# Two-block transformer kernel: both delta-rule chains of the mixer in the same beats, and the gated unit's first channel between the two sixes of query, key and value slabs

## The chip, the cores and the metric

One core of a Trainium2 chip runs the whole program. The metric is the device time of one execution in microseconds (us), the median over runs. The engines are named as the profile names them: PE (TensorE, matrix products), PEld (its weight loads), DVE (VectorE), ACT (ScalarE), POOL (GpSimd) and SP (SyncE, which issues the DMAs).

## The reference, cut to what matters

Input x is 512 tokens of 1024 features, float32. Two blocks follow one another. The first is a hybrid mixer, a cross attention to 256 memory tokens and a gated feed-forward net with a short convolution; the second is a retention layer and a stick-breaking attention layer. The change is in the mixer of the first block only:

```python
z = h @ w_in                                    # qkv (1536), gate, a/b logits, cfm_in (1024)
qkv = silu(causal_dwconv(qkv, gdn_conv_w))      # 4 taps, 12 tiles of 128 features
q, k = l2norm(q), l2norm(k)                     # 4 heads of 128
g = -exp(a_log) * softplus(a_logit + dt_bias); beta = sigmoid(b_logit)
o = gated_delta_rule_chunked(q, k, v, g, beta)  # chunks of 64 tokens:
#   L = strict(beta k k^T * decay); solve (I + L) [u | w] = [beta v | beta k exp(g)]
#   for each of 8 chunks: v_new = u - w S;  o = q exp(g) S + (q k^T * decay) v_new
#                         S = S exp(g_last) + (k exp(g_last - g))^T v_new
o = rmsnorm(o, gdn_norm_g) * silu(gate)
c = causal_dwconv(glu(cfm_in), cfm_dw_w) + cfm_dw_b     # 31 taps, 4 channels of 128 features
c = silu(layernorm(c))
y = concat([o, c]) @ w_out
```

## The kernel before, in words

**Products.** Activations lie with features on partitions and the 512 tokens along the free axis. Every float32 weight slab (128 x 1024, 512 KB) is brought in by SP through three `raw` buffers, rounded to a high part by ACT (`sh`, line 1307) and split into a low part by DVE (`sl`, line 2052), in four slots each. A product of a slab is then three passes (lines 502 to 504) over eight feature tiles, 24 matmuls of 512 columns. The helper `slab` does one slab, `tokens` does four slabs with tokens as the stationary side; small float32 products go through `one` (line 507).

**Order of the work.** It is written out by hand, once for each engine, in `tensor_program`, `scalar_program`, `vector_program` and `pool_program`. An order list (`weight_order`) fixes which slab comes when: slabs 0 to 5 are query, key and value of heads 0 and 1, slabs 6 to 9 the gated unit's channels 0 and 1 (two slabs each), slabs 10 to 15 query, key and value of heads 2 and 3, slabs 16 to 19 the gated unit's channels 2 and 3, slabs 20 to 31 the eight memory-key and four gate slabs in the order of `KEYS_GATES`, slabs 32 to 39 the memory values, slabs 40 to 47 the output projection of the mixer.

**Beats and lanes.** Work other than slabs is written as Python generators that are put into lanes (`bg`, `fg`, `side`; `gp` and `tp` for the 31-tap convolution). At each beat every lane runs its first generator on to the next `yield`. When a generator ends, the next one in its lane starts within the same tick. On PE a slab has three beats (after 9, 18 and 24 of its 24 matmuls), a memory-key slab one, a group of `tokens` two (for two token tiles). Each of the other engines has its own beats written at matching places; the engines meet through semaphores alone, each engine running its own list strictly in order.

**The chains.** `chain(p)` does the delta rule of heads 2p and 2p+1; it takes 37 ticks on PE: k k^T (tick 2), the transposes of v (5 and 6), q k^T and the start of the inverse (7), five doubling levels of two ticks each (8 to 17: 16 products of 64x64 in the first, 32 in the second), keys, u and w (18 to 20), then for each of 8 chunks a tick with w S (`ws`) and one with k^T v_new and the output (`kv`, `o`) (21 to 36), and the transposes back (37, line 820). Chain 0 starts before slab 6 in lane `bg`, chain 1 after slab 14 in lane `fg`. The state `SS` is one tile for both; POOL zeroes it again for chain 1 (line 3063). Each chain has two PSUM banks of its own, `KBANK = ((4, 5), (2, 3))`; the recurrence uses banks 6 and 7 in turn for `ws` and `o`, and one of the chain's own for `kv`. ACT copies each chunk's output out of PSUM (`tok`, line 1458).

**The 31-tap convolution.** Channels 0 and 2 are done by ACT (products, line 1503) and POOL (sums, line 3071). Channels 1 and 3 are done by DVE (lines 2257 and 2262), one tap at each beat of DVE in lane `tp`, two at each beat from the memory keys on, 31 taps each; taps(1) is added behind glu(1), taps(3) behind glu(3). `cfm_norm` is the layer norm behind it. Before the second beat group of the memory values has its split, `tp` is drained.

**The heads' norm.** `gdn_out(p)` has on ACT the squares of the output (first tick, line 1582) and the logarithm and exponential (fourth tick, lines 1590 and 1594); it has five yields there. On DVE it has the sum of squares (second tick, line 2376) and the scaling (sixth tick, line 2381), and six yields. On PE it has a product with ones for each head (third tick), and three yields. gdn_out(0) is added to lane `side` at item 10 of `KEYS_GATES`, gdn_out(1) to lane `fg` after item 11, before the memory values.

Of the kernel before, what the change touches and what calls it, by code (L numbers as in the profile page):

```python
# [9 lines left out]
ALU = mybir.AluOpType  # L10
# [5 lines left out]
EPS = 1e-6  # L16
# [150 lines left out]
def program(nc, A, out):  # L167
    root = ExitStack()
    with root:
# [42 lines left out]
        with ExitStack() as ph:  # L212
# [14 lines left out]
            SS = alloc(ph, "ss", [128, 2, 128])  # L227
# [189 lines left out]
        def tap_sum(c, q):  # L417

            return ACC[:, c, :] if q == 30 else PS[TAP_BANKS[0] if c == 1 and q < TAP_HOP else TAP_BANKS[1]][:]
# [36 lines left out]
        GLB = ((1, 2), (0, 1), (0, 1), (0, 1))  # L456
# [31 lines left out]
        def tensor_program(e):  # L488
# [127 lines left out]
            for _ in range(8):  # L616
                one(PS[7][:, 0:256], SS[:, 0, :], SS[:].rearrange("p a b -> p (a b)"), True, True)

# [67 lines left out]
            def chain(p):  # L686
# [103 lines left out]
                for n in range(8):  # L790
                    tb, par = n // 2, n % 2
                    R, RO = RR[par], RR[1 - par]
                    b = bank(6 + par)
                    pe.wait_ge(*gac[(p, "wq", par)])
                    pe.wait_ge(*(gdv[(p, "s", n - 1)] if n else ggp[(p, "s0")]))
                    for h in range(2):
                        g = (h * 8 + n) * 128
                        t = one(b[:, h * 128:h * 128 + 128], W2[:, g:g + 128], SS[:, h, :], h == 0, False)
# [24 lines left out]
                rel[6], rel[7] = [(gac, (p, "ot", 0))], [(gac, (p, "ot", 1))]  # L823

            def mem():
                b = bank(3)
# [6 lines left out]
                rel[3] = [(ms, "mem")]  # L833
# [3 lines left out]
                one(bank(3)[:, 0:256], ONE[:], DG[:, 0:256], True, True).then_inc(*rw("mem"))  # L837
                rel[3] = [(rb, "mem")]
# [9 lines left out]
            bg.add(chain(0))  # L848

# [18 lines left out]
            rel[TAP_BANKS[1]] = [(tpd, (3, 30))]  # L868
# [37 lines left out]
            fg.drain()  # L906
            fg.add(gdn_out(1))
# [2413 lines left out]
```

## Time and profile before

| | |
|---|---|
| median of 3 runs | 1692.43 us (1691.57 to 1696.03) |
| time of the profiled execution | 1691.26 us |
| its span, first to last instruction | 1689.5 us |
| PE busy | 1673.6 us (99%) in 9421 matmuls |
| PE weight loads | 1404.4 us (83%) |
| DVE busy | 1047.3 us (62%) |
| ACT busy | 739.1 us (44%) |
| POOL busy | 187.3 us (11%) |
| mean granted clock of PE | 0.999 of full speed |

The span is that of the one profiled execution; its own time is 1.8 us more. Busy times of PE are modelled: matmuls overlap in the pipeline, so the distance between the starts of two matmuls says more than their lengths. A line x16 or x32 can hold two records for each small float32 product. The number in brackets at a line's end is the idle time before it and what ended it.

### The profile page before, as it was taken

How to read it: one execution, taken by the hardware profiler on the slowest of the kernel's cores; microseconds unless marked ns; L12 is line 12 of the kernel's file. 1: busy time of each engine (PE TensorE's matmuls, PEld its weight loads, DVE VectorE, ACT ScalarE, POOL GpSimd, SP SyncE). 2: the span in 40 equal slices, each digit the busy share in tenths (PEclk: the TensorE clock that was granted, in tenths of full speed). 3: DMA queues.
4: the chain of work that ended last, by engine and by line, in shares of the span. 5: the costliest groups of instructions: out<-in, count | busy, mean ns of one | idle time of the engine just before them, and what ended most of it. 6: DMA issues, size and time to landing. Idle time of an engine off the chain costs nothing.

```text
span 1689.5 us, 23254 instructions
## 1 busy us (share of the span) xinstructions
PE 1673.6 (99%) x9421; PEld 1404.4 (83%) x9421; DVE 1047.3 (62%) x1565; ACT 739.1 (44%) x1137; POOL 187.3 (11%) x163
## 2 busy tenths in 40 slices
PE   9999999999999999999999999999999999999998
PEld 7787887987898888888888888888898888888887
DVE  7889787474389449549675642655574545454445
ACT  6654467653553323213543323323364645253463
POOL 0455461200200000000100000000100000000001
PEclk9999999999999999999999999999999999999999
DMA  6111134421223223322322313313222222222221
GB/s 216 62 43 63 51 101 135 137 78 50 75 67 121 100 75 113 101 86 100 119 88 80 96 56 106 100 57 112 69 72 76 75 76 87 75 87 76 85 77 50
DMA packets 45576, 147.67 MB, mean 87 GB/s; under 512 B 5024, under 2 KB 8992, under 8 KB 45472
## 3 DMA queue, kind: packets, MB, share of 16 engines
q1 hardware_dynamic: 45472, 146.21, 26.5%
q8 instruction: 75, 1.23, 0.3%
q14 instruction: 29, 0.24, 0.0%
HBM read 144.09 MB, written 2.10 MB: 87 GB/s over the span
## 4 chain that ended last, share of the span: by engine, by line
PE 88%; DVE 8%; ACT 2%; issue 1%; DMA 0%; POOL 0%; SPq 0%; DVEq 0%; ACTq 0%
PE ps L502 22%; PE ps L504 22%; PE ps L503 22%; PE ps L507 21%; DVE sl L2052 1%; DVE ps L2112 1%; DVE y L2467 1%; DVE xl L2484 1%; DVE h L2477 0%; PE ps L1128 0%; ACT sh L1307 0%; DVE ps L2262 0%; DVE ps L2106 0%; DVE pad L2104 0%; DMA raw<-in_wqkv 0%
## 5 line engine op out<-in xcount | busy, mean ns | idle before, releaser
L1307 ACT ACTIVATE sh<-raw 128x1024 fp32r<-128x1024 f32 x257 | 268.3, 1053 | 373.1 <-PE ps L504 254.4
L2052 DVE TENSOR_TENSOR sl<-raw,sh 128x1024 fp32r<-128x1024 f32 x257 | 321.6, 1258 | 131.5 <-ACT sh L1307 131.4
L502 PE MATMUL ps<-xh,sh 128*128 128x512 f32 (+1 forms) x664 | 263.1, 396 | 0.0
L504 PE MATMUL ps<-xl,sh 128*128 128x512 f32 (+1 forms) x664 | 254.0, 382 | 0.0
L503 PE MATMUL ps<-xh,sl 128*128 128x512 f32 (+1 forms) x664 | 253.7, 382 | 0.0
L502 PE MATMUL ps<-sh,xh 128*128 128x512 f32 x384 | 151.8, 395 | 0.0
L503 PE MATMUL ps<-sh,xl 128*128 128x512 f32 x384 | 149.6, 390 | 0.0
L504 PE MATMUL ps<-sl,xh 128*128 128x512 f32 x384 | 149.6, 390 | 0.0
L502 PEld LDWEIGHTS ps<-xh,sh 128*128 128x128 f32 x664 | 124.9, 188 | 26.2 <-issue 2.4
L504 PEld LDWEIGHTS ps<-xl,sh 128*128 128x128 f32 x664 | 124.8, 188 | 24.9
L503 PEld LDWEIGHTS ps<-xh,sl 128*128 128x128 f32 x664 | 125.0, 188 | 22.7 <-issue 0.7
L3002 POOL TENSOR_TENSOR dg<-dg,sq 128x512 f32<-128x512 f32 (+1 forms) x27 | 30.1, 1116 | 828.4 <-ACT sq L1313 827.2
L502 PE MATMUL ps<-x2hu,sh 128*128 128x256 f32 (+1 forms) x346 | 118.4, 342 | 0.0
L504 PE MATMUL ps<-x2lu,sh 128*128 128x256 f32 (+1 forms) x346 | 115.8, 335 | 0.0
L503 PE MATMUL ps<-x2hu,sl 128*128 128x256 f32 (+1 forms) x346 | 115.1, 333 | 0.0
L502 PE MATMUL ps<-x2hd,sh 128*128 128x512 f32 (+1 forms) x300 | 103.7, 346 | 0.1
L504 PE MATMUL ps<-x2ld,sh 128*128 128x512 f32 (+1 forms) x300 | 102.4, 341 | 0.0
L503 PE MATMUL ps<-x2hd,sl 128*128 128x512 f32 (+1 forms) x300 | 102.1, 340 | 0.0
L3071 POOL TENSOR_TENSOR acc<-acc,ca 128x512 f32<-128x512 f32 x60 | 86.0, 1433 | 68.9 <-ACT ca L1503 64.5
L504 PEld LDWEIGHTS ps<-sl,xh 128*128 128x128 f32 x384 | 72.1, 188 | 15.6
L502 PEld LDWEIGHTS ps<-sh,xh 128*128 128x128 f32 x384 | 72.1, 188 | 15.2 <-issue 0.5
L503 PEld LDWEIGHTS ps<-sh,xl 128*128 128x128 f32 x384 | 72.1, 188 | 15.2 <-issue 0.5
(429 smaller groups left out, 3317.5 us busy)
## 6 DMA issues: line engine op xcount, KB each, us to landing
raw<-in_wup SPq DMA_DIRECT2D x44, 512.0 KB, 3.5
raw<-in_wdn SPq DMA_DIRECT2D x24, 512.0 KB, 3.5
raw<-in_rqk SPq DMA_DIRECT2D x16, 512.0 KB, 3.9
raw<-in_rv SPq DMA_DIRECT2D x16, 512.0 KB, 3.4
raw<-in_rg SPq DMA_DIRECT2D x16, 512.0 KB, 4.4
raw<-in_rout SPq DMA_DIRECT2D x16, 512.0 KB, 3.5
raw<-in_sv SPq DMA_DIRECT2D x16, 512.0 KB, 3.4
raw<-in_sg SPq DMA_DIRECT2D x16, 512.0 KB, 3.5
```

The lines of the kernel that those rows point to most:

```text
L502: e.matmul(dst, wh, ah, start=start, stop=False, skip_group_check=True)
L503: e.matmul(dst, wl, ah, start=False, stop=False, skip_group_check=True)
L504: return e.matmul(dst, wh, al, start=False, stop=stop, skip_group_check=True)
L507: return e.matmul(dst, a, b, start=start, stop=stop, skip_group_check=True)
L1307: e.activation(SH[j % NSPL][:], RAW[j % NRAW][:], ACT.Copy).then_inc(*hi(j))
L2052: e.tensor_tensor(SL[j % NSPL][:], RAW[j % NRAW][:], SH[j % NSPL][:].bitcast(F32), ALU.subtract).then_inc(*lo(j))
L2112: e.scalar_tensor_tensor(C[:], PAD[:, 1 + q:1 + q + T], prm("gconv", tile * 4 + q), C[:], ALU.mult, ALU.add).then_inc(*cv((n, "t", q) if q ...
L2467: e.scalar_tensor_tensor(Y[:, k, c], Y[:, k, c], prm(gpost[0], gpost[1] + k), PS[0][:, 0:256] if b == 5 and hf else YR[:, c], ALU.mult, AL ...
L2484: e.scalar_tensor_tensor(lo_[:, k, c], H[:, k, c], prm(g[0], g[1] + k), hi_[:, k, c].bitcast(F32), ALU.mult, ALU.subtract).then_inc(*s2((k ...
L3002: e.tensor_tensor(SA[:, c], SA[:, c], SQ[(k - 1) % 2][:] if k < 4 else half(SQ, k % 4), ALU.add).then_inc(*sa(("y", b, k)))
L3071: e.tensor_tensor(ACC[:, c, :], ACC[:, c, :], gpb[("tmp", c, q)], ALU.add).then_inc(*tpp((c, q)))
```

## The change

Both chains are added to their lanes at the same place, after slab 12 (`JOIN = 10`, the slab of the conv tile n = 10). The gated unit's channel 0 keeps slabs 6 and 7; channel 1 moves behind the second six, which move two slabs forward (slabs 8 to 13; glu(1) has 14 and 15). Each chain has a state of its own, zeroed at the start. `ws` and `o` use the chain's own second bank for every chunk in place of banks 6 and 7 in turn. The DVE taps have one bank, 7, and no change of bank. The memory's sums move from bank 3 to 6. The chains are drained, and both gdn_out are put into lane `side`, at item 9 of `KEYS_GATES` (`HEADS_OUT = 9`). Nothing is computed otherwise than before.

```diff
 weight_order:
-        for c in (2 * p, 2 * p + 1):
+        for c in ((0,), (1, 2, 3))[p]:
             o += [("wcfm", 4 + c), ("wcfm", c)]
...
-            SS = alloc(ph, "ss", [128, 2, 128])
+            SSP = [alloc(ph, f"ss{i}", [128, 2, 128]) for i in range(2)]
...
-        ONB = ((4, 3), (6, 7))
-        TAP_BANKS, TAP_HOP = (2, 5), 12
-        CVB = (0, 1, 2, 3, 5, 0, 0, 1, 0, 1, 0, 1)
+        ONB = ((4, 5), (2, 3))
+        TAP_BANK, JOIN, HEADS_OUT = 7, 10, 9
+        CVB = (0, 1, 2, 3, 5, 0, 1, 0, 1, 0, 1, 0)
-        GLB = ((1, 2), (0, 1), (0, 1), (0, 1))
+        GLB = ((1, 0),) * 4
 PE, chain(p):
-                    b = bank(6 + par)
+                    b = bank(B_)
...
-                    rel[6 + par] = [(gac, (p, "tok", n))]
+                    rel[B_] = [(gac, (p, "tok", n))]
                     yield
                 for h in range(2):
-                    b = bank(6 + h)
+                    b = bank(KBANK[p][h])
 PE, main order:
-            bg.add(chain(0))
             glu(0, 6)
             side.add(mem())
-            glu(1, 8)
-            rel[TAP_BANKS[0]] = [(tpd, (1, TAP_HOP))]
             for n in range(6, 12):
-                slab(4 + n, X, "x", beats=3, at_bank=[n % 2])
-                rel[n % 2] = [(cva, conv_tile(n))]
-                if n == 10:
+                slab(n + 2, X, "x", beats=3, at_bank=[CVB[n]])
+                rel[CVB[n]] = [(cva, conv_tile(n))]
+                if n == JOIN:
+                    bg.add(chain(0))
                     fg.add(chain(1))
+            glu(1, 14)
             glu(2, 16)
             glu(3, 18)
...
-            bg.drain()
             side.drain()
             for i, (kind, n) in enumerate(KEYS_GATES):
-                if i == 10:
+                if i == HEADS_OUT:
+                    bg.drain()
+                    fg.drain()
                     side.add(gdn_out(0))
+                    side.add(gdn_out(1))
...
-            fg.drain()
-            fg.add(gdn_out(1))
             bg.add(cfm_norm())
 ACT and DVE: the same moves of chain, glu(1), gdn_out and drains
 DVE, taps(c):
+                        ve.wait_ge(*dca[("ea", 1, 1)])
...
-                        if c == 1 and q == TAP_HOP:
-                            ve.wait_ge(*gac[(0, "w", 1)])
 POOL:
-            e.memset(SS[:], 0.0).then_inc(*ggp((0, "s0")))
+            e.memset(SSP[0][:], 0.0).then_inc(*ggp((0, "s0")))
+            e.memset(SSP[1][:], 0.0).then_inc(*ggp((1, "s0")))
...
-                if p:
-                    po.wait_ge(*gdv[(0, "s", 6)])
-                    po.wait_ge(*gmm[(0, "o", 7)])
-                    e.memset(SS[:], 0.0).then_inc(*ggp((1, "s0")))
```

## Rows read from the trace of the kernel before

**Rows 1.** The page, part 1: busy time, share of the span and instructions of each engine.

```profile
PE 1673.6 (99%) x9421; PEld 1404.4 (83%) x9421; DVE 1047.3 (62%) x1565; ACT 739.1 (44%) x1137; POOL 187.3 (11%) x163
```

**Rows 2.** Waits of PE: who waited for whom; us in total, times, longest.

```profile
PE ps L706 <- DVE u_xq L2167: 1.3, 1, 1.3
PE ps L507 <- DVE km L2179: 1.1, 1, 1.1
...
PE ps L820 <- ACT qk L1458: 0.9, 2, 0.6
```

**Rows 3.** PE timeline: a stretch of slabs alone; start, length, engine, line, operation, tiles.

```profile
41.09 0.39 PE L502 MATMUL ps<-xh,sh 128*128 128x512 f32 x1
...
44.27 0.39 PE L504 MATMUL ps<-xl,sh 128*128 128x512 f32 x1
```

**Rows 4.** PE timeline: chain 0's doubling levels between pieces of slabs.

```profile
79.96 1.15 PE L507 MATMUL ps<-u_xq,u_x 64*64 64x64 f32 x32
...
83.30 1.15 PE L507 MATMUL ps<-km,u_xq 64*64 64x64 f32 x32
84.29 1.10 PE L507 MATMUL ps<-u_xq,km 64*64 64x64 f32 x32
...
86.91 1.15 PE L507 MATMUL ps<-u_xq,u_x 64*64 64x64 f32 x32
```

**Rows 5.** PE timeline: chain 0's recurrence alone, then sharing a beat with chain 1.

```profile
120.33 0.61 PE L507 MATMUL ps<-ss,u_xq 128*128 128x128 f32 x4
...
122.96 0.71 PE L507 MATMUL ps<-qk,u_x 64*128 64x128 f32 x4
...
126.38 0.60 PE L507 MATMUL ps<-ss,u_xq 128*128 128x128 f32 x4
...
152.50 0.71 PE L507 MATMUL ps<-qk,u_x 64*128 64x128 f32 x4
...
153.71 0.66 PE L706 MATMUL ps<-idn,u_rq 128*128 128x128 f32 x4
```

**Rows 6.** DVE timeline: the first operations of two successive convolution tiles.

```profile
24.37 0.69 DVE L2104 TENSOR_TENSOR pad<-ps,rb 128x512 f32<-128x512 f32 x1 [1.56 <-ACT rb L1387]
...
29.27 0.68 DVE L2104 TENSOR_TENSOR pad<-ps,rb 128x512 f32<-128x512 f32 x1
```

**Rows 7.** POOL timeline: one of the chain's masks.

```profile
65.09 1.30 POOL L3045 TENSOR_TENSOR u_l<-u_a,ch 128x512 f32<-128x512 f32 x1
```

**Rows 8.** ACT timeline: one copy of a chunk's output.

```profile
240.05 0.38 ACT L1458 ACTIVATE qk<-ps 64x256 f32<-64x256 f32 x1 [1.04 <-PE ps L507]
```

**Rows 9.** DVE timeline: two taps, and the operations around the start of the memory values.

```profile
242.42 1.53 DVE L2262 SCALAR_TENSOR_TENSOR ps<-cp,prm,ps 128x512 f32<-128x512 f32 x2
...
263.95 0.42 DVE L2408 TENSOR_TENSOR km<-ps,cm 128x256 f32<-128x256 f32 x1
264.30 1.21 DVE L2052 TENSOR_TENSOR sl<-raw,sh 128x1024 fp32r<-128x1024 f32 x1
267.61 1.30 DVE L2376 TENSOR_TENSOR sq<-sq,q 128x512 f32<-128x512 f32 x2 [2.09 <-ACT sq L1582]
268.82 0.74 DVE L2381 SCALAR_TENSOR_TENSOR qk<-qk,prm,dg 128x512 f32<-128x512 f32 x1
...
271.28 0.68 DVE L2389 TENSOR_TENSOR gt<-qk,gt 128x512 f32<-128x512 f32 x1
```

**Rows 10.** Windows at the end: us, PE, PEld, DVE, ACT, POOL busy, PEclk, DMA share, GB/s.

```profile
1685.50:1686.00 0.50, 0.05 (x1) 0.00 (x0) 0.50 (x3) 0.38 (x1) 0.00 (x0) 1.00 1.03 342
...
1687.00:1689.47 2.47, 0.00 (x0) 0.00 (x0) 0.00 (x0) 0.00 (x0) 0.00 (x0) 0.50 0.63 211
```

**Rows 11.** PE timeline: the eight float32 products (256 columns) at the start, two later.

```profile
1.10 5.25 PE L507 MATMUL ps<-ss 128*128 128x256 f32 x16 [1.10 <-POOL ss L3017]
...
326.25 0.59 PE L507 MATMUL ps<-dg,one 128*128 128x256 f32 x2
326.68 0.59 PE L507 MATMUL ps<-sq,one 128*128 128x256 f32 x2
```

More of the change, by code:

```diff
@@ L417, in tap_sum @@
         def tap_sum(c, q):
-            return ACC[:, c, :] if q == 30 else PS[TAP_BANKS[0] if c == 1 and q < TAP_HOP else TAP_BANKS[1]][:]
+            return ACC[:, c, :] if q == 30 else PS[TAP_BANK][:]
         RS = (DG[:], PAD[:, 0:T])
@@ L616, in tensor_program @@
             for _ in range(8):
-                one(PS[7][:, 0:256], SS[:, 0, :], SS[:].rearrange("p a b -> p (a b)"), True, True)
+                one(PS[7][:, 0:256], SSP[0][:, 0, :], SSP[0][:].rearrange("p a b -> p (a b)"), True, True)
             for i, k in FIRST:
@@ L797, in chain @@
                         g = (h * 8 + n) * 128
-                        t = one(b[:, h * 128:h * 128 + 128], W2[:, g:g + 128], SS[:, h, :], h == 0, False)
+                        t = one(b[:, h * 128:h * 128 + 128], W2[:, g:g + 128], SSP[p][:, h, :], h == 0, False)
                     t.then_inc(*gmm((p, "ws", n)))
@@ L822, in chain @@
                 yield
-                rel[6], rel[7] = [(gac, (p, "ot", 0))], [(gac, (p, "ot", 1))]
+                rel[A_], rel[B_] = [(gac, (p, "ot", 0))], [(gac, (p, "ot", 1))]
             def mem():
-                b = bank(3)
+                b = bank(6)
                 for _ in range(9):
@@ L836, in mem @@
                 pe.wait_ge(*dg["mem"])
-                one(bank(3)[:, 0:256], ONE[:], DG[:, 0:256], True, True).then_inc(*rw("mem"))
-                rel[3] = [(rb, "mem")]
+                one(bank(6)[:, 0:256], ONE[:], DG[:, 0:256], True, True).then_inc(*rw("mem"))
+                rel[6] = [(rb, "mem")]
                 yield
@@ L1523, in scalar_program @@
             ahead(10)
-            bg.add(chain(0))
+            conv_act(4)
+            beat(3)
+            conv_act(5)
             def glu(c, j):
-                if c == 0:
-                    conv_act(4)
-                beat(2 if c == 2 else 3)
+                beat(2 if c < 2 else 3)
                 ahead(j + 5)
-                if c == 0:
-                    conv_act(5)
                 ac.wait_ge(*glv[(c, "sg")])
@@ L1541, in scalar_program @@
             side.add(mem())
-            glu(1, 8)
             for n in range(6, 12):
                 beat(2 if n > 6 else 3)
-                ahead(9 + n)
-                if n == 10:
+                ahead(n + 7)
+                if n == JOIN:
+                    bg.add(chain(0))
                     fg.add(chain(1))
@@ L1549, in scalar_program @@
                 conv_act(n)
+            glu(1, 14)
             glu(2, 16)
@@ L1608, in mem_v @@
                                  ACT.Copy, scale=LNC[:, 2 + tb:3 + tb]).then_inc(*vma((cg, tb)))
-            bg.drain()
             side.drain()
             for i, (kind, n) in enumerate(KEYS_GATES):
-                if i == 10:
+                if i == HEADS_OUT:
+                    bg.drain()
+                    fg.drain()
                     side.add(gdn_out(0))
+                    side.add(gdn_out(1))
                 if kind == "mk":
@@ L2236, in mem @@
                 ve.wait_ge(*cs["m"])
-                e.tensor_scalar(LNC[:, 0:2], PS[3][:, 0:2], 1.0 / 1024, EPS, ALU.mult, ALU.add).then_inc(*ms("mem"))
+                e.tensor_scalar(LNC[:, 0:2], PS[6][:, 0:2], 1.0 / 1024, EPS, ALU.mult, ALU.add).then_inc(*ms("mem"))
                 yield
@@ L2301, in glu @@
             def glu(c, j):
-                beat(3 if c % 2 else 2)
+                beat(2 if c < 2 else 3)
                 ve.wait_ge(*used[j])
@@ L2324, in vector_program @@
             side.add(mem())
-            glu(1, 8)
             for n in range(6, 12):
                 beat(2 if n > 6 else 3)
-                if n == 10:
+                if n == JOIN:
+                    bg.add(chain(0))
                     fg.add(chain(1))
-                conv(n, 4 + n, n % 2, beat)
-                low(8 + n)
+                conv(n, n + 2, CVB[n], beat)
+                low(n + 6)
+            glu(1, 14)
             glu(2, 16)
@@ L2395, in head_lo @@
                     *x2l(("2mix", k)))
-            bg.drain()
             side.drain()
             for i, (kind, n) in enumerate(KEYS_GATES):
-                if i == 10:
+                if i == HEADS_OUT:
+                    bg.drain()
+                    fg.drain()
                     side.add(gdn_out(0))
+                    side.add(gdn_out(1))
                 if kind == "mk":
@@ L3088, in pool_program @@
             beat(3)
-            bg.add(chain(0))
-            for c in range(2):
+            for c in range(4):
+                if c == 1:
+                    for n in range(6, 12):
+                        beat(3)
+                        if n == JOIN:
+                            bg.add(chain(0))
+                            fg.add(chain(1))
                 beat(6)
@@ L3095, in pool_program @@
                     gp.add(taps(c))
-            for n in range(6, 12):
-                beat(3)
-                if n == 10:
-                    fg.add(chain(1))
-            for c in (2, 3):
-                beat(6)
-                if c in ON_GP:
-                    gp.add(taps(c))
-            bg.drain()
             side.drain()
```

21 lines of the change are left out of this document (9 added, 12 removed).

## The prediction

> **What bounds the kernel now.** I read the page first: PE is busy for 99% of the span [rows 1], so a time can only come from PE's own work growing or shrinking, or from holes. The view of waits, taken for PE alone, shows how small the holes are: the longest is 1.3 us, where the chain's second transposes wait for DVE; then 1.1 us for the start of the inverse, and 0.9 us at the transposes back [rows 2]. Then I read PE's timeline through the mixer, for the distances between starts. In a slab alone 14 steps take 44.27 - 41.09 = 3.18 us [rows 3], 0.227 us for each 512-column matmul; nine between two beats take 2.04. Whatever a beat takes beyond that is what its chain work costs, the change from one kind of product to the other included.
>
> **Part 1: sharing beats saves changes.** A first half of a level costs 83.30 - 79.96 - 2.04 = 1.30 us. A second half has 6 matmuls behind it (1.36): 86.91 - 83.30 - 1.36 = 2.25 [rows 4]. Within that beat the second set of 16 products starts 0.99 us after the first, so a set costs 0.99 when it follows another and the rest, 0.27 to 0.31, is entering and leaving float32. With both chains in a beat that rest is paid once: 10 level beats by 0.29 = 2.9 us. In the recurrence `ws` costs 122.96 - 120.33 - 2.04 = 0.59, `kv` and `o` together 126.38 - 122.96 - 2.04 = 1.38; where chain 1's transposes follow `kv` and `o` in the same beat, they start after 153.71 - 152.50 = 1.21 [rows 5]. So 8 beats by 0.17 = 1.4. For `ws` no such pair is used here; it lies between nothing and 0.17, nearer nothing, since two wide float32 products fill most of the 0.59: 8 by 0.05 = 0.4. The other eight beats (k k^T, two of transposes, q k^T, keys, u, w, back) lie between 0.1 and 0.3: 8 by 0.17 = 1.4. Together 6.1. But seven beats are shared already, chain 0's last and chain 1's first; by the same prices they now save 7 by 0.2 = 1.4. And three pieces of side work (decay rows, a memory sum) ride in chain 0's beats now and stand alone after: 3 by 0.2 = 0.6. **Saved: 6.1 - 1.4 - 0.6 = 4.1 us**, bounds 2.5 and 6.
>
> **Part 2: slabs ahead of the chains.** Slabs 8 to 13 come one behind another and alternate between banks 0 and 1, so slab n+2 waits for the convolution of slab n. DVE takes 29.27 - 24.37 = 4.90 us for a convolution and a split [rows 6], PE 24 by 0.227 = 5.45 for a slab. The eight memory splits (a quarter of a slab's split each, under 0.5 us) come in the first three of these slabs and take the margin away: three slabs by 4.9 + 1.3 against 5.45 is 2.3 us behind, of which DVE's head start of under two us is taken off. **0.5 us lost**, bounds 0 and 1.5. The DMAs keep order and number; only four slabs change places with six others, and the issue on SP hangs on the splits as before. Losing POOL's second zeroing and its two waits costs nothing: it is done at the start, ahead of the first product.
>
> **Part 3: the chains' start, twice in the same beats.** The two waits of 1.3 and 1.1 us [rows 2] come from DVE and POOL working through norms, masks and scaling between ticks 2 and 7. Now both chains ask for that at once. POOL's masks double (a mask is 1.30 [rows 7]), DVE's chain work (seven operations on a 512-column tile at 0.68 [rows 9] and some small ones, about 5.5 us) becomes 11, beside one convolution and two splits, 4.9 + 1.2 [rows 6]. PE has, from k k^T to the inverse, five pieces of slab (about 10.2) and 4 to 5 us of chain work. There are no taps on DVE at that time, since taps(1) starts behind glu(1); that is the cover. I get PE to the second transposes 1.9 us early and to chain 1's inverse 0.7 early. 2.6 us lost against 2.4 for chain 0 and about 0.8 for chain 1 now: **0.6 us won**, bounds 2 won and 3 lost.
>
> **Part 4: one bank for `ws` and `o`.** Before, `ws` of a chunk needed the copy of two chunks ago, now that of the last. The copy takes 0.38 [rows 8] and there is a piece of slab of 2.04 us, or a memory-key slab, between `o` and the next `ws`. ACT reaches the copy in time except where a Silu of a gate tile stands ahead of it, which waits for DVE, which has six taps to do: I take **0.7 us lost** in all, bounds 0 and 14 waits by 0.5, 7.
>
> **Part 5: the end of the chains.** Both have done 36 ticks by item 9 and the last one is drained without a slab over it; ACT copies chain 0's output between chain 0's transposes back and chain 1's. About 1.5 us, where now two waits at the transposes, 0.9 together [rows 2], and one of 0.5 before them stand. Nothing, within 1.
>
> **Part 6: gdn_out(0) and gdn_out(1) in one lane.** This is the dear one. In one lane the second starts when the first has ended, and the first is three yields long on PE and six on DVE. Count ticks from item 9: items 9, 10, 11 have 1, 3, 1, so the memory values start with tick 6. PE's product for gdn_out(1) is in tick 3 + 3 = 6, after the first six matmuls of slab 32. DVE's sum of squares, which it needs, is in tick 6 + 2 = 8, in the second group. PE stands in order and waits. Behind the end of slab 31 DVE still has: the evacuation of item 11, 0.42; a split, 1.2; gdn_out(0)'s scaling, 2 by 0.7; four taps (channel 3's are not through: 12 + 16 + 24 = 52 of 62 taps fit before), 2 by 1.45; a split, 1.2; head_out(0), 0.6; the first sum, 0.65 [rows 9]. That is 8.4 us. PE has six matmuls to do in that time, 1.36. **7.0 us lost**, bounds 6.5 (DVE quite up to date when slab 31 ends) and 8.5 (it is over a us late). Before, both generators started at the same beat on every engine, and no wait is seen there. Nothing gives it back later: the ten taps moved to this place (7.3 us of DVE) are then hidden under the wait, and without the wait they would not be free either.
>
> **Part 7: the clock.** PE's last product ends at 1685.55, and from 1687.0 on the granted clock is 0.50, half of 2.4 GHz [rows 10]; so a hole of 7 us should see it fall. What it costs to come back: the eight first products take 5.25 us, and two such products later start 326.68 - 326.25 = 0.43 apart, 3.4 for eight [rows 11]. **1.8 us lost**; bounds 0 (it does not fall) and 2.6 (all 5.25 at half speed). The Trainium skill says the same from the other side: "TensorE: Matmul & The Clock Gate", under "Why this matters for your kernels", warns against idle gaps between bursts of matmuls since the clock then drops. By that rule the sum stands; if it did not hold for this hole the sum would be 1.8 less.
>
> **The sum.** -4.1 + 0.5 - 0.6 + 0.7 + 0 + 7.0 + 1.8 = +5.3 us. Against the profiled execution's own 1691.26 that is 1696.6; that execution lies 1.2 under the median of 1692.43, so I forecast 1692.4 + 5.3 = **1697.7 us**, 0.31% slower. A measurement of this kernel can tell about 0.3%, 5.1 us, from no change; my sum stands just on that line.
>
> **Rivals.** (a) *The clock holds* through the hole: +3.5, 1695.9, within 0.3%. Against it stands the fall 1.45 us after the last product [rows 10]. (b) *No hole:* DVE reaches tick 8 in time, or the two lanes' counts meet by something that I misread; then parts 6 and 7 go and the result ends on the other side, -3.5, 1688.9. It decides at the third group of six matmuls in slab 32: if PE passes it without a wait, this is the case. For it speaks only that waits now are small everywhere. If the sharing saved its upper bound too, it would be -5.4, 1687.0. (c) *Waits all through the shared beats:* each `ws` waits for a copy just asked for, each `kv` for DVE, which has up to two taps and both chains to serve in a beat of a memory-key slab (about 4.2 us of work for 4.2 to 5.6 of PE). 14 bank turns by 0.5 less the 0.7 counted: +11.6, 1704. Against it: ACT waits 1.04 us for PE just before such a copy [rows 8], so it is not behind there. The Trainium skill would point here: "Trainium Kernel Development and Optimization", "Best Practices", reads regular bubbles as a sign that PSUM buffers ran out, and this change halves them for `ws`. No bubble is seen with two banks, so the trace cannot decide it.
>
> **Chances.** The forecast's mechanism with the clock falling 0.50, of it 0.32 above 5.1 and 0.18 below; (a) 0.14, all within; (b) 0.20, of it 0.11 beyond 5.1 with savings at their bound and 0.09 within; (c) 0.16, all slower. So slower 0.48, within 0.3% 0.41, faster 0.11. The range goes from 1688.5 (no hole, savings as taken) to 1703 (the forecast and half of (c)); beyond it lie the better half of (b) and the worse half of (c).
>
> **What would show it.** In the changed trace: x32 groups of both chains 0.99 apart in the same beat; PE's view of waits led by one of about 7 us, the product with ones (line 507, `sq`, `one`) waiting for DVE line 2376's tile, just after the start of the memory values; the granted clock below 1 in the window behind it; PE reaching slab 32 some 3 to 4 us earlier than now if parts 1 to 5 are right. I am wrong in part 6 if that wait is under 3 us, in part 1 if the start of slab 32 has not moved forward, in part 4 if waits on line 1458 add up to more than 2 us.

## The result, and the profile after

The changed kernel takes **1728.74 us** (median of 4 runs, 1727.64 to 1732.31) against 1693.32 (1691.57 to 1696.03) of the kernel before on the same chip: ratio 1.0216, 95% interval 1.0205 to 1.0228. It is 2.2% slower, 35 us, where 5 us were forecast. The direction was right, the size was not, and the time lies far outside the range.

The page of the changed kernel, its span, part 1 and two rows of part 2; it answers to [rows 1].

```profile
span 1727.6 us, 23250 instructions
PE 1683.4 (97%) x9421; PEld 1415.1 (82%) x9421; DVE 1055.1 (61%) x1565; ACT 745.7 (43%) x1142; POOL 183.3 (11%) x163
PE   9889997999999999999999999999999999999998
PEclk9999898999999999999999999999999999999999
```

The profiled span grew by 1727.6 - 1689.5 = 38.1 us. PE has the same 9421 products but is busy 9.8 us longer, and idle 28.3 us longer. Everything happens in slices 2 to 8, the mixer; two digits of the clock's row are 8 there, and no slice of the kernel before shows less than 9. So two things have to be found: idle time and a slower clock.

The view of waits for PE alone; us in total, times, longest. It answers to [rows 2].

```profile
PE ps L507 <- DVE sq L2371: 9.1, 1, 9.1
PE ps L502 <- ACT u_xq L1395: 5.0, 1, 5.0
PE ps L706 <- DVE u_xq L2164: 4.3, 1, 4.3
PE ps L820 <- ACT qk L1456: 3.3, 2, 2.2
PE ps L507 <- DVE sl L2049: 2.7, 5, 1.0
PE ps L502 <- DVE cp L2312: 2.6, 1, 2.6
PE ps L502 <- ACT qk L1395: 2.1, 1, 2.1
PE ps L507 <- DVE dg L2054: 1.5, 1, 1.5
PE ps L507 <- DVE sq L2356: 1.5, 1, 1.5
...
PE ps L507 <- DVE u_t L2176: 1.0, 1, 1.0
PE ps L507 <- POOL msum L3073: 1.0, 1, 1.0
```

The first row is the hole that was predicted at gdn_out(1), 9.1 us instead of 7.0. The second (slab 7 waits for the Silu of convolution 5), the sixth (slab 20 waits for DVE's work on slab 19, channel 3 of the gated unit) and the seventh (a slab waits for a convolution's Silu) are turns of a PSUM bank in the slabs; of these the prediction has only the last one's kind, at 0.5 us. The third is the chains' start, the fourth their end.

The granted clock is best read in windows laid on the stretches where it is at 0.50, here with one of 1.00 ahead of the third (columns: window, length, PE, PEld, DVE, ACT, POOL busy, PEclk, DMA share, GB/s).

```profile
61.90:65.30 3.40, 3.40 (x8) 2.72 (x9) 0.00 (x0) 2.80 (x3) 0.00 (x0) 0.51 0.32 130
120.20:126.80 6.60, 5.65 (x17) 4.41 (x17) 5.92 (x8) 2.95 (x3) 6.31 (x5) 0.50 0.26 79
191.00:195.00 4.00, 4.00 (x40) 3.56 (x39) 0.41 (x1) 1.04 (x2) 1.26 (x1) 1.00 0.36 126
195.40:205.40 10.00, 9.76 (x43) 8.76 (x42) 0.55 (x2) 6.83 (x12) 1.82 (x2) 0.50 0.00 1
209.00:212.00 3.00, 3.00 (x16) 3.00 (x15) 0.00 (x0) 0.00 (x0) 0.94 (x1) 0.50 0.59 180
273.60:276.80 3.20, 3.03 (x14) 3.04 (x15) 1.21 (x2) 1.80 (x6) 0.00 (x0) 0.50 0.54 169
300.30:304.20 3.90, 3.89 (x5) 1.83 (x6) 3.76 (x6) 0.00 (x0) 0.00 (x0) 0.50 0.32 122
```

The clock falls to 1.2 GHz, half of 2.4, six times. PE works in these windows for 3.4 + 5.7 + 9.8 + 3.0 + 3.0 + 3.9 = 28.8 us; at half speed about half of that, **14.4 us**, is lost. Now the balance closes: 28.3 us of idle time and 14.4 of clock make 42.7, and the span grew by 38.1, so the sharing of beats saved about **4.6 us**.

Five of the falls stand at a wait. The third does not. PE's timeline there (start, length, engine, line, operation, tiles) shows `w` of chain 0 and, right behind it, `w` of chain 1:

```profile
191.88 3.06 PE L507 MATMUL ps<-km,u_xq 64*128 64x64 f32 x29
...
195.05 5.55 PE L507 MATMUL ps<-u_t,u_rq 64*128 64x64 f32 x29
```

29 products of the same shape took 3.06 us and then 5.55, with PE never idle.

**Where the sharing did save.** PE's timeline in a level of both chains, which answers to [rows 4]:

```profile
134.59 1.15 PE L507 MATMUL ps<-u_xq,u_x 64*64 64x64 f32 x32
135.57 1.10 PE L507 MATMUL ps<-u_rq,u_r 64*64 64x64 f32 x32
...
138.19 1.15 PE L507 MATMUL ps<-km,u_xq 64*64 64x64 f32 x32
139.17 1.10 PE L507 MATMUL ps<-u_xq,km 64*64 64x64 f32 x32
140.10 1.10 PE L507 MATMUL ps<-u_t,u_rq 64*64 64x64 f32 x32
```

Two sets start 0.98 and 0.93 apart. The pair of first halves costs 138.19 - 134.59 less six wide products (1.36) = 2.24, where twice 1.30 was paid.

### The profile page after: what moved, and what is told of

Its sections match the earlier page's. It is cut to its first block, busy times and chain, and to the rows that moved or that the text cites. A ratio compares the mean times of both kernels' runs of the same rounds, so it can differ in the third digit from the quotient of the medians.

```text
span 1727.6 us, 23250 instructions
## 1 busy us (share of the span) xinstructions
PE 1683.4 (97%) x9421; PEld 1415.1 (82%) x9421; DVE 1055.1 (61%) x1565; ACT 745.7 (43%) x1142; POOL 183.3 (11%) x163
## 4 chain that ended last, share of the span: by engine, by line
PE 84%; DVE 9%; ACT 3%; issue 2%; DMA 0%; SPq 0%; POOL 0%; DVEq 0%; ACTq 0%; POOLq 0%
PE ps L502 21%; PE ps L504 21%; PE ps L503 21%; PE ps L507 20%; DVE sl L2049 2%; DVE ps L2109 1%; DVE y L2462 1%; DVE ps L2258 1%; DVE xl L2479 1%; ACT sh L1305 1%; DVE h L2472 0%; PE ps L1126 0%; DMA acc<-in_xT 0%; DVE ps L2103 0%; DVE u_xq L2085 0%
## 5 line engine op out<-in xcount | busy, mean ns | idle before, releaser
L504 PEld LDWEIGHTS ps<-sl,xh 128*128 128x128 f32 x384 | 72.1, 188 | 15.7
```

The source lines that it names most:

```text
L504: return e.matmul(dst, wh, al, start=False, stop=stop, skip_group_check=True)
```

## The experiments

PE's idle time at each place and the clock give the candidates; each of these kernels takes one away. The first five are each one edit of the changed kernel.

**1. gdn_out(1) in its old lane.** The same edit on PE, ACT and DVE:

```diff
                     side.add(gdn_out(0))
-                    side.add(gdn_out(1))
...
                 rel[i % 2] = [(kmv if kind == "mk" else gtv, n)]
+            fg.add(gdn_out(1))
             bg.add(cfm_norm())
```

> The changed kernel, with gdn_out(1) put back into lane fg behind item 11 on PE, ACT and DVE, so that its ticks are counted alike again. In the changed kernel PE waited 9.1 us for it and the clock was at half for 10.2 us from that wait on. My theory: the wait was the lanes' miscount and nothing else, so the time falls by 9.1 for the wait and 1 to 2 for the clock, to about 1718. Rival: DVE is late there anyhow, with ten taps moved in, and the wait comes back under the names of splits and sums; then it falls by 2 to 4 only, to about 1725.

Measured: 1727.91 us (1723.51 to 1728.49), ratio to the kernel before 1.0204 (1.0189 to 1.022). By the ratios that is 0.12%, 2 us, and the intervals overlap: removing the largest hole is worth next to nothing. The waits of PE from the memory values to the output projection in this kernel:

```profile
PE ps L507 <- DVE u_l L2342: 4.8, 1, 4.8
PE ps L507 <- DVE sq L2371: 1.6, 1, 1.6
PE ps L502 <- DVE km L2404: 1.2, 1, 1.2
```

The hole is gone and 7.6 us stand elsewhere: DVE is behind, and PE now meets that at the channel sums (line 2342). So the lane's count decided where PE stopped, not how long. What makes DVE late there is a separate question; run 8 is about it.

**2. Slab 7 in bank 2, as before.**

```diff
-        GLB = ((1, 0),) * 4
+        GLB = ((1, 2),) + ((1, 0),) * 3
```

> The changed kernel, with the second slab of the gated unit's channel 0 in bank 2 as before, in place of bank 0. Theory: its wait of 5.0 us for ACT's Silu of convolution 5 goes, and with it the fall of the clock for 3.4 us behind it (1.7 us of work), so 6 to 7 us less, about 1722. Rival: the stretch of slabs 8 to 13 is bound by DVE and the wait only moves to their banks; then at most 2 us less, about 1727.

Measured: 1727.10 (1724.52 to 1727.74), 1.0202 (1.0187 to 1.0218). The 5.0 us wait is gone and the chains start 4.8 us earlier (k k^T at 102.06 instead of 106.86), but in the profiled run the clock stays at half for 17 us around `w` instead of 10, and about half of the gain is lost there.

**3. The memory's split and sums behind slab 13.** `side.add(mem())` goes from ahead of convolution 6 to behind convolution 11 on all four engines.

```diff
             glu(0, 6)
-            side.add(mem())
             for n in range(6, 12):
...
+            side.add(mem())
             glu(1, 14)
```

> The changed kernel, with the memory's norm started behind slab 13 and not before slab 8, on all engines. Theory: between slabs 8 and 13 DVE is full with convolutions and splits, and the memory's work makes PE wait 1.0 + 1.5 us by itself and 2.1 us at a bank; these go, but part of it comes back at the start of the chains, where DVE is behind already: 2 to 4 us less, about 1726. Rival: it comes back whole, 1729 or more, since the chains' start waits for DVE and POOL more than slabs 8 to 13 do.

Measured: 1726.69 (1726.05 to 1729.06), 1.0205 (1.019 to 1.0221). The chains start 6.3 us earlier (100.59): the 2.1, 1.5 and 1.0 us waits in slabs 8 to 13 are gone, and PE's own memory products have moved behind slab 13 as well. About half of it comes back: the second transposes wait 5.3 us instead of 4.3, the start of the inverse 1.5 instead of 1.0, and the memory's diagonal costs 1.4 at its new place.

**4. Both lanes drained in turns** instead of chain 0 and then chain 1.

```diff
-                    bg.drain()
-                    fg.drain()
+                    while bg.todo or fg.todo:
+                        bg.tick()
+                        fg.tick()
```

> The changed kernel, with the two chains drained by turns (one tick each) in place of one after the other, on PE, ACT and DVE. Theory: chain 1's last copy no longer stands behind chain 0's transposes on ACT, so that of the 3.3 us of waits at the transposes back about 1.5 go: 1727. Rival: the waits are ACT's two splits and taps ahead of the copies and stay; 1729, no change.

Measured: 1727.78 (1726.74 to 1728.32), 1.0208 (1.0191 to 1.0225). Of the two waits at the transposes back (2.2 and 1.1) the second is gone. It is 1 us, less than the runs can tell.

**5. Chain 1 one beat behind chain 0**, on every engine, by a generator that yields once first.

```diff
-                    fg.add(chain(1))
+                    fg.add(later(chain(1), 1))
```

> The changed kernel, with chain 1 one beat behind chain 0 on every engine (one empty tick ahead of it). Every beat still holds work of both. Theory A: the clock falls at 195 us since the two w products of 64 by 64 and 128 columns follow one another for 8.6 us without a slab between them; with a piece of slab between them it does not fall there, about 4 us less, and the wait of 4.3 us at the second transposes gets smaller by 1 to 2; one more tick is drained without cover, 1 us more. Together 1723. Theory B: the clock there answers to the sum of chain work over the whole stretch; no gain from it, 1728 to 1730.

Measured: 1725.81 (1723.89 to 1727.02), 1.0204 (1.0186 to 1.0221). Over the beats of `w` the window's clock is 1.00:

```profile
190.00:210.00 20.00, 20.00 (x168) 17.81 (x167) 9.86 (x18) 11.12 (x20) 7.01 (x5) 1.00 0.09 28
```

The recurrence starts 6.4 us earlier (196.90 against 203.25; part of that only because w(1) now comes after it), and the wait at the second transposes is 3.4 instead of 4.3. But by the ratios the total moves 0.12%, 2 us; the balances behind run 13 show what was lost against it.

**6 and 7. Edits 1 to 4 together, and these with the stagger.**

> The changed kernel with the first four edits together (heads' lane, bank 2, memory behind slab 13, drains by turns). If the four losses are separate they add: 10.5 + 6.5 + 3 + 1.5 = 21.5 less, 1707. If DVE bounds the whole mixer, so that a wait taken away in one place returns in the next, it stays above 1713.

> The same with chain 1 one beat behind chain 0 besides. Theory A of that edit: 4 to 5 us under the run without it, about 1702. Theory B: the same as without it, within 2 us.

Measured: 1714.86 (1711.81 to 1715.17), 1.0132 (1.0117 to 1.0147), and 1712.95 (1711.41 to 1714.16), 1.0125 (1.011 to 1.014). By the ratios the four edits alone are worth 0.12, 0.14, 0.11 and 0.08%, none of them clear of the noise; together they are worth 0.84%, more than their sum of 0.45%. The surplus is not in the waits. In the profiled executions PE is idle 3.9, 5.0, 2.6 and 0.0 us less in runs 1 to 4, 11.5 in all, and 12.7 less in run 6. It is in the clock: the time lost at half clock is 2.2 and 2.7 us more in runs 1 and 2, 1.3 and 2.4 less in runs 3 and 4, and 5.1 less in run 6. Why the clock falls less often once all four waits are gone, no run shows. In run 6 the 4.8 us at the channel sums are still there.

**8. The lane of run 1, and the 62 taps through before the memory values**, by two DVE taps in a beat of channels 2 and 3:

```diff
             def glu(c, j):
-                beat(2 if c < 2 else 3)
+                taps_ = 2 if c > 1 else 1
+                beat(2 if c < 2 else 3, taps_)
...
-                beat(3)
+                beat(3, taps_)
```

> The change, with gdn_out(1) back behind the last gate in the other lane, and with two taps in a beat of VectorE's in the glu of channels 2 and 3, so that the 62 taps are through before the memory values. With the lane alone (the earlier run) the hole of 9.1 us went and 4.8 + 1.6 + 1.2 us of other waits came, and the stretch from the memory tokens to the output projection still took 36.2 us where the kernel before took 25.4. Theory: the ten taps pushed into this stretch are what is left, so with them gone the waits there fall under 2 us, the stretch takes 25 to 29 us and the time is 1716 to 1720 us. Rival: the taps were free there, or cost as much in the glu beats; then the stretch or what is before it keeps the time and the whole is within 2 us of 1727.9.

Measured: 1718.72 (1717.05 to 1720.71), 1.016 (1.0146 to 1.0174). Here the theory held in the time and in the stretch. The stretch of the memory values, in windows of the kernel before, of the changed one and of this one:

```profile
266.00:292.00 26.00, 26.00 (x110) 20.14 (x109) 22.98 (x31) 18.90 (x31) 0.00 (x0) 1.00 0.45 139
```

```profile
289.00:328.00 39.00, 28.39 (x110) 20.73 (x109) 34.37 (x46) 22.80 (x30) 0.13 (x1) 0.87 0.31 99
```

```profile
290.00:316.00 26.00, 25.87 (x106) 19.62 (x107) 24.75 (x33) 22.48 (x30) 0.00 (x0) 1.00 0.47 156
```

The number behind PEld's is DVE's. Before it had 23.0 us of work under 26.0 of PE. The changed kernel puts 12 taps (9.05 us) on top, so DVE needs 34.4, and PE takes 39. Run 1 still has the 12 taps there, 33.8 us of DVE and 36 of PE. With the taps gone as well DVE has 24.8, and the stretch fits into 26 again (315.70 - 289.91 = 25.8 from the first product of the memory values to the first of the output projection; 25.4 before, 38.5 changed). The taps found room in the beats of channels 2 and 3 at little cost: the memory values start at 289.91 instead of 289.57, though the wait at slab 20 is 3.4 us instead of 2.6. Over all the kernels of this study the same stretch takes 38.1 to 38.5 us with the 12 taps and both gdn_out in one lane, 35.4 to 36.3 with the taps and the old lane, and 25.7 to 25.8 with the old lane and no taps. A kernel without the taps but with both gdn_out in one lane was not measured.

**9. All tables of banks as before.**

```diff
-        CVB = (0, 1, 2, 3, 5, 0, 1, 0, 1, 0, 1, 0)
+        CVB = (0, 1, 2, 3, 5, 0, 0, 1, 0, 1, 0, 1)
...
-        GLB = ((1, 0),) * 4
+        GLB = ((1, 2), (0, 1), (0, 1), (0, 1))
```

> The change with the kernel before's tables of banks (slab 7 in bank 2; channels 1 to 3 of the gated unit in banks 0 and 1 in that order, convolutions 6 to 11 in 0, 0, 1, 0, 1, 0 turned to 0, 1, 0, 1 behind slab 8). Theory: the waits of 5.0 us (slab 7 for the Silu of convolution 5) and of 2.6 us (bank 0 asked for by two slabs in a row) go, and with them a fall of the clock or two: 1719 to 1723 us. Rival: the slabs behind wait as much longer for VectorE, which is late there anyway, and the time is within 2 us of 1727.1, the time with slab 7's bank alone.

Measured: 1722.29 (1720.4 to 1723.7), 1.018 (1.0166 to 1.0194). Both waits, 5.0 and 2.6, are gone. The second is the same mistake in another place: with (1, 0) channel 3 leaves slab 19 in bank 0, and slab 20, the first of the memory keys, takes bank 0 too, so its first product waits for DVE to have done with slab 19 (line 2312). The order (0, 1) puts slab 19 in bank 1. By the ratios the time is 0.22%, 3.7 us, under run 2's, of which 2.6 are the wait; for the rest there is the clock, which in this run's profile is at half for 10 us around `w` and not for 17.

**10 and 11. All repairs, and with the stagger.** Edits 1, 3, 4, 8 and 9 together.

> All repairs that leave both chains in the same beats: the banks of before, the memory sums behind slab 13, the drain of both lanes in turns, gdn_out(1) in the other lane, and the 62 taps through before the memory values. Theory (each cost is its own): 1714.9 of the earlier sum of repairs, less 8 to 10 for the taps, less 2 to 4 for the second bank wait: 1701 to 1705 us, still above the kernel before, since both chains' start (4 to 5 us of waits) and the clock's fall in w (10 us at half) stay. Rival: what is repaired comes out as waits elsewhere, since VectorE is what is late: 1709 or more.

> The same as the run before, with chain 1 one beat behind chain 0, so that w of both chains no longer stands back to back. Theory: no clock at half in the w beats, 3 to 5 us less there, 2 us lost again by a longer tail of the chains: 1699 to 1703 us. If it comes out under 1692 the sharing of beats would pay once its side effects are repaired; I do not expect it. Rival: the stagger only moves the waits (the earlier pair differed by 1.9 us): within 1 us of the run before.

Measured: 1701.67 (1700.11 to 1702.65), 1.0058 (1.0044 to 1.0072), and 1703.57 (1702.76 to 1705.24), 1.0073 (1.006 to 1.0085). So of the change's 2.16% the edits around the shared beats take back 1.58%, 27 us, and 0.58%, 10 us, stay. PE's waits in run 10:

```profile
PE ps L706 <- DVE u_xq L2166: 5.3, 1, 5.3
...
PE ps L820 <- ACT qk L1457: 2.2, 1, 2.2
PE ps L507 <- DVE u_t L2178: 1.5, 1, 1.5
PE ps L507 <- DVE dg L2056: 1.4, 1, 1.4
```

The chains' start (5.3 + 1.5, against 1.3 + 1.1 in [rows 2]) and their end are left, and the clock in `w`:

```profile
186.80:196.80 10.00, 10.00 (x48) 9.30 (x47) 0.30 (x1) 6.20 (x11) 1.27 (x1) 0.50 0.00 1
```

The last two kernels are edits of run 10's.

**12. w(1) alone one beat later**, on the base of run 10: chain 1 yields once more between `u` and `w` on PE, ACT and DVE.

```diff
                 yield
+                if p:
+                    yield
                 for par in range(2):
                     b = bank(KBANK[p][par])
```

> The sum of repairs (1701.7 us) with chain 1 one beat behind from its w on, and level with chain 0 before that. Theory: the clock falls in the w beats because both chains' u and w products stand close together; with w(1) one beat later the granted clock stays whole there (10.2 us at half in the sum of repairs), which is 4 to 5 us of PE's time, less about 0.5 to 1 us since ws(0) of chain 1, its transposes back and one ws/o pair no longer share: 1697 to 1699 us. Rival: the fall comes from what is done before, or from the total of such work; then it comes as well, or 10 us later, and the time is 1701 to 1703.

Measured: 1702.3 (1700.03 to 1705.28), 1.0061 (1.0048 to 1.0074): no change. The windows show the clock whole over u, w(0) and what follows, and then one shorter fall behind w(1), again with PE never idle:

```profile
183.30:192.30 9.00, 8.90 (x75) 8.07 (x74) 4.88 (x8) 3.73 (x7) 2.53 (x2) 1.00 0.16 56
192.40:195.80 3.40, 3.40 (x18) 3.40 (x18) 1.16 (x2) 3.32 (x6) 0.51 (x1) 0.54 0.33 96
```

So the long fall comes with the two `w` close together: 10.0 us at half became 3.4, some 3.3 us of PE's time. It was mostly spent again: from w(0) to the first transposes back only 1.0 us is gained (74.5 for 75.5), so 2.3 went into chain 1's recurrence no longer pairing with chain 0's, kind by kind; and the tail from there to the memory values takes 1.1 more (16.9 for 15.8). The theory was right on the cause and wrong on the time.

**13. Both chains one slab later**, on the base of run 10, so that convolution 11 is out of their way:

```diff
-        TAP_BANK, JOIN, HEADS_OUT = 7, 10, 9
+        TAP_BANK, JOIN, HEADS_OUT = 7, 11, 10
```

> The sum of repairs (1701.7 us) with both chains' start one slab later, with the first slab of channel 1, so that convolution 11 and its split are ahead of them and only the gated unit's work stands beside them. The items before the drain are ten instead of nine. Theory: of the 5.3 us wait at the second transposes about half is convolution 11 and the split (5.3 to 2.5), the waits of 1.5 and 1.4 behind it stay: 3 us less, against 1 to 2 us for two more ticks drained with little over them: 1700 to 1702. Rival one, the start is bound by both chains' own small operations beside GpSimd: the wait stays above 4 us and the time is 1703 or more. Rival two, the slabs ahead catch up nothing: same wait, later.

Measured: 1704.84 (1701.62 to 1706.55), 1.0072 (1.0059 to 1.0086). The wait is 4.2 instead of 5.3, the one of 2.2 at the transposes back goes, and two new ones of 2.1 and 2.3 come. The time is what the first rival expected. DVE's timeline ahead of the transposes:

```profile
105.44 1.25 DVE L2154 TENSOR_TENSOR smp<-smp 128x8 f32<-128x8 f32 x1
106.62 0.15 DVE L2155 TENSOR_TENSOR smp<-smp 128x8 f32<-128x8 f32 x1
...
107.44 1.22 DVE L2161 TENSOR_TENSOR smp<-smp,smv 128x8 f32<-128x8 f32 x1
...
108.66 1.01 DVE L2155 TENSOR_TENSOR smp<-smp 128x8 f32<-128x8 f32 x1
...
109.90 1.12 DVE L2161 TENSOR_TENSOR smp<-smp,smv 128x8 f32<-128x8 f32 x1
```

These are eight operations on eight columns, 5.5 us from the first to the end of the last, four of them over 1 us and three 0.15 to 0.17 (the eighth 0.59). The two chains' scaling of norms is stretched here too. The run does not isolate it: convolution 11 is out of the way, but the memory's splits, which start at the same slab, now stand beside it (three before the first transposed tile, 0.87 for two and 1.33 for one). And run 13's idle time is 0.6 us under run 10's; what makes it slower in the profile is the clock.

**The balance of every kernel.** Idle time is what PE is idle more than in the kernel before; clock is half of PE's work in windows laid over each whole fall (for the changed kernel 14.9, where the narrower windows above gave 14.4); what these two exceed the growth of the span by is saved. All in us, from the profiled executions.

| kernel | span | idle time | clock | saved |
|---|---|---|---|---|
| changed | +38.1 | 28.3 | 14.9 | 5.1 |
| runs 1, 2, 3, 4 | +37.2, 36.0, 34.7, 36.6 | 24.5, 23.4, 25.8, 28.4 | 17.1, 17.6, 13.6, 12.5 | 4.4, 5.1, 4.8, 4.3 |
| runs 6, 8, 9, 10 | +20.5, 25.7, 31.8, 10.8 | 15.7, 16.6, 20.8, 7.5 | 9.8, 13.8, 16.3, 8.8 | 5.1, 4.7, 5.3, 5.5 |
| run 13 | +13.1 | 6.9 | 13.0 | 6.8 |
| runs 5, 7, 11 (stagger) | +32.5, 21.0, 12.2 | 24.4, 14.6, 7.1 | 9.3, 9.0, 6.2 | 1.1, 2.6, 1.2 |
| run 12 (w(1) later) | +10.5 | 8.1 | 5.2 | 2.8 |

The last column is a remainder, but a steady one: 4.3 to 5.5 us in nine of the ten kernels whose chains go level, 1.1 to 2.8 where chain 1 is a beat behind, all along or from `w` on. So the stagger gives back clock (2.6 us from run 10 to run 11) and loses most of what sharing beats had saved (4.3 us).

No kernel of this study is faster than the kernel before.

## Why the prediction was wrong

**Part 1 (sharing saves 4.1 us, bounds 2.5 to 6) was right.** The price of [rows 4] carries over, 2.24 for a pair of first halves, and the balance of the span gives 4.6 us. By the prediction's own sign it would be wrong: the start of slab 32 has not moved forward, it comes at 289.57 us instead of 266.00. But that sign holds the costs of parts 2 to 5 and of the clock too, and these are what moved it; the sign was badly chosen. In run 10 the same balance gives the same: idle time grew by 7.3 us over the kernel before, PE did about 17 us of work at half clock (3.4 at 56.8, 3.4 behind the transposes, 10 in `w`), 8.4 lost, and the span is 10.7 longer, so 5.0 saved.

**Part 2 (slabs ahead, 0.5 us) is the step that failed first.** It counted only DVE and named slabs 8 to 13. That slab n+2 waits for the convolution of slab n was right, but the part never looked at who frees slab 7's bank. With (1, 0) slab 7 takes bank 0 from slab 5, whose reader is ACT's Silu of convolution 5, and that stands behind decay's exponentials and a table load. ACT's timeline of the changed kernel:

```profile
59.30 0.63 ACT L1419 ACTIVATE u_a<-u_a 128x512 f32<-128x512 f32 x1
59.95 1.28 ACT L1395 ACT_TABLE_LOAD   x1
61.24 0.60 ACT L1395 ACTIVATE u_xq<-ps 128x512 f32<-128x512 f32 x1
```

PE starts slab 7 at 61.89 after 4.97 us. The diff's line on GLB has no term in the prediction; it was one of its own, 5.0 us at slab 7 and 2.6 at slabs 19 and 20, and the clock behind each. In slabs 8 to 13 the estimate of the memory's splits ("under 0.5 us" each) was low. DVE's timeline there:

```profile
73.55 1.22 DVE L2229 SCALAR_TENSOR_TENSOR x2lu<-gt,prm,x2hu 128x256 fp32r<-128x256 f32 x1 [0.83 <-ACT x2hu L1478]
...
93.19 2.03 DVE L2049 TENSOR_TENSOR sl<-raw,sh 128x1024 fp32r<-128x1024 f32 x1
95.14 1.49 DVE L2054 TENSOR_TENSOR dg<-idn,lnc 128x256 f32<-128x256 f32 x1
```

Single splits take up to 1.22, a slab's split up to 2.03 (1.22 elsewhere), and the memory's diagonal 1.49; the estimate had none of that, though in the kernel before two of the eight memory splits take 1.52 and 1.56 us where five take 0.47 or 0.48. From the first of these slabs to k k^T PE waits 2.1 + 1.5 + 1.0 us, the last of them for POOL's memory sum. Run 3 prices it: with the memory's work out of the way the chains start 6.3 us earlier, of which these waits are 4.6 and the rest is PE's own work, which moved along.

**Part 3 (the start, 0.6 us won, bounds 2 won and 3 lost).** The mechanism was named and the sign was wrong: 4.3 + 1.0 us of waits stand where 2.4 and chain 1's 0.8 stood, 2.1 lost, inside the bounds; the clock's fall behind them, 5.7 us of work at half, adds 2.8, and with it the term is outside. That DVE's chain work of "about 5.5 us" becomes 11 left out that small operations stretch. DVE's timeline in the kernel before shows one already, with the split ahead of it:

```profile
60.56 1.87 DVE L2052 TENSOR_TENSOR sl<-raw,sh 128x1024 fp32r<-128x1024 f32 x1
62.35 1.25 DVE L2155 TENSOR_TENSOR smp<-smp 128x8 f32<-128x8 f32 x1
```

In the changed kernel three of eight take 1.00, 1.26 and 0.97 us and the others 0.16 or 0.17; and the split behind them takes 1.85. The stretched ones stand beside a POOL operation of 1.04 to 1.3 us. The Trainium skill ("SBUF — State Buffer", "Who interferes with whom") says that a DVE instruction with two inputs in SBUF contends with a GpSimd instruction that reads SBUF, and calls their shared ports an exclusive lock. The rows agree: an operation of 0.16 us becomes one of 0.97 to 1.26, longer by about one POOL operation. That it is this, no run here shows by itself, since POOL's work was in none of them moved off. Starting both chains at once puts twice the work on both sides.

**Part 4 (one bank for `ws` and `o`, 0.7, bounds 0 and 7) came out near its lower bound.** There is one wait of 0.2 us for such a copy in the whole recurrence. The prediction's sign, over 2 us of waits on that line, does show, but 3.3 of the 3.5 us stand at the transposes back, which are part 5. Rival (c), waits all through the shared beats, is wrong: the recurrence was never the problem.

**Part 5 (the end, nothing within 1)** was too low: 2.2 + 1.1 us of waits stand for the 0.9 + 0.5 of before, and a fall of the clock takes 1.5 us more: 3.3 + 1.5 - 1.4 = 3.4 lost. Run 4 takes away 1.1 of it.

**Part 6 (7.0 us, bounds 6.5 and 8.5) was right in its place, its kind and nearly its size.** The wait stands at the product of `sq` with ones; DVE's timeline shows the operations that were listed:

```profile
291.92 0.42 DVE L2405 TENSOR_TENSOR km<-ps,cm 128x256 f32<-128x256 f32 x1
292.25 1.22 DVE L2049 TENSOR_TENSOR sl<-raw,sh 128x1024 fp32r<-128x1024 f32 x1
...
...
299.48 1.29 DVE L2371 TENSOR_TENSOR sq<-sq,q 128x512 f32<-128x512 f32 x2
```

From 291.92 until PE goes on at 300.31 they take the 8.4 us that were counted. The bound was still too low: PE starts slab 32 at 289.57 and DVE comes to slab 31's evacuation only at 291.92, 2.3 us late, where the bound had "over a us late". 8.4 + 2.3 less some 1.5 of PE's own work is the 9.1. What failed is the last sentence: "the ten taps moved to this place are then hidden under the wait". They are 12, and they are not hidden under it but a cause of it, and of more behind it: the stretch lost 13.1 us (38.5 against 25.4), not 7.0 + 1.8. The same sentence said that without the wait the taps would not be free either, and run 1 bears that out, at 10.8 us (36.2 against 25.4), not the 7.3 of their work. With the lane put back the stretch loses 10.8 us, with the taps gone as well (run 8) 0.4: the taps are by far the larger term.

**Part 7 (the clock, 1.8 us, one fall).** For the fall that it speaks of it was right: 3.9 us of work at half is 1.95 lost. It was wrong to count one: there are six, 14.4 us. Five of them come with waits of 2.2 us and more, the dearest without one. Not every such wait brings one: behind the 2.2 us at the transposes back in run 10 the clock stays whole. The Trainium skill's rule that was quoted there ("TensorE: Matmul & The Clock Gate", "Why this matters for your kernels") speaks of idle gaps. For the holes the trace agrees; at `w` the clock fell with PE busy for all of the 4 us before (191 to 195), and there the measurement decides.

In one sum: sharing -4.6; idle time in slabs 7 to 20, bank turns and memory work, +12.2 (5.0, 2.6, 2.1, 1.5, 1.0); at the chains' start and end +5; behind them +11 (9.1, 1.5 and a 1.0 that stands for one of 0.4); clock +14.4. That is 38, the growth of the span. Between 50 and 345 us PE is idle for 32.9 us, against 5.3 in the kernel before.

Against the prediction's terms the missing 33 us are 12.6 of clock (part 7), 11.7 in the slabs (part 2), 5.4 at the chains' start and end (parts 3 and 5) and 4.2 at the memory values (part 6), less 1.2 (parts 1 and 4). The direction was right with a better reason than luck, since the hole was there; but the prediction made the hole the whole loss, and rival (b) put the kernel without it at 1688.9 us. Run 1 is that kernel, and it takes 1727.91.

**What stays open.** The 10.7 us by which run 10's span is longer are 4.4 of waits at the start (5.3 + 1.5 for 2.4), 1.3 at the end (2.2 for 0.9), 1.4 for the memory's diagonal and 8.4 of clock, less the 5.0 saved. That POOL's contest with DVE makes the start long was not tried. The kernel before starts chain 0 alone beside the gated unit, and all these costs lie under other work there; whether a start apart and a meeting later would keep both gains was not tried either.

## What to carry to other kernels

When a change puts two chains into the same beats, what they share on the bottleneck is the small term; first work out what each other engine must now deliver in the same few microseconds, stretch by stretch, as its busy time over the bottleneck's (23.0 under 26.0 held, 34.4 under 26.0 cost 13 us). Read every changed bank table as a wait: name the last reader of that bank, its engine, and what stands ahead of it in that engine's order. And do not expect removing the largest wait to give back its length: the first repair, of a wait of 9.1 us, gave 2 us by the ratios, and with the taps 9.5.

## What the runs showed of the hardware that was not expected

- The granted clock fell to 1.2 GHz while PE was busy without a gap: in the second of two neighbouring `w` sets (64 rows in, 64 columns, float32; 3.06 and then 5.55 us for 29 products), for 10 us. The nine other kernels that keep the two sets together show it too, in these beats or just behind them, five of them for 10 us (3.4 to 17 in all; in some a part stands behind the wait at slab 20). With the two a beat apart (runs 5, 7, 11, 12) it stayed whole or fell for 3.4 us, and with one chain alone (the kernel before) it stayed whole. In run 10 it fell once more with PE busy throughout:

```profile
56.00:60.00 4.00, 4.00 (x13) 3.08 (x12) 3.88 (x8) 2.44 (x5) 1.27 (x1) 0.60 0.35 111
```

  Behind PE there lay again a set of small float32 products (decay's, 16 rows each, at 53.7 us). It fell at the same place in runs 2, 9 and 12, but not in runs 6, 7, 11 and 13 nor in the kernel before, which have the same products there. So a busy PE can lose its clock, and what decides it is open.
- Executions of code that is the same up to a point differ by a piece of 3.4 us at half clock, so two kernels compared by one profile each can differ by 1.7 us for no reason in the code (at slab 7 the clock is at half for 3.4 us in the changed kernel and for 6.8 in run 1, and k k^T comes at 106.86 and at 108.12).
- DVE operations on 128x8 take 0.16 us alone and 0.97 to 1.26 where POOL works beside them, and a split 1.2 alone and 1.5 to 2.0.
